# The chunked two-way scan of a recurrent mixer moved to four quadrants of the array, with its five operand products on GpSimd

## Chip, cores, metric

One core of a Trainium2 chip runs the whole network in one launch. The metric is the device time of that launch in microseconds (us). PE is TensorE (PEld its weight loads), DVE is VectorE, ACT is ScalarE, POOL is GpSimd, SP issues the DMAs.

## The reference, cut to what matters

The program is a network of several blocks. The edit lies in one mixer of the second part, an RWKV-7 style recurrence over 256 context and then 512 latent tokens, 8 heads of 64, once forward and once backward:

```
def _rwkv7_scan(S0, r, w, k, v, kk, a):
    def step(S, inp):
        r_t, w_t, k_t, v_t, kk_t, a_t = inp
        sa = jnp.einsum('bhvk,bhk->bhv', S, kk_t)
        S = (S * w_t[:, :, None, :] - sa[..., None] * (kk_t * a_t)[:, :, None, :]
             + v_t[..., None] * k_t[:, :, None, :])
        return S, jnp.einsum('bhvk,bhk->bhv', S, r_t)
```

`yf_l` and `yb_l` of the two directions are added, normalised per head, and gated. Everything is fp32.

## The kernel before, in words

`rwkv_prepare` computes the decays' running sums (`cum`), the normalised keys (`kk`) and their negative product with `a` (`b_neg`) for all 769 columns (256, a gap, 512). `rwkv_scan` then goes over 12 chunks of 64 tokens in each direction, and `rwkv_finish` adds, normalises and gates. Each is a phase of its own, with a barrier at its ends.

In the scan the 8 heads lie as 4 column groups (`q`) by two halves of 64 partitions. A matmul of one head has 64 rows, 64 columns and 64 moving columns, and in fp32 it is two instructions in the trace. `heads` puts the two halves' heads on the two diagonal quadrants of the array: rows 0 to 63 write to partitions 0 to 63, rows 64 to 127 to partitions 64 to 127.

A chunk of one direction is a chain of steps, in the list `order`:

- ScalarE `grown`: the exponentials of the running sum and of its negative (`own`, `grow`, L2697, L2698); `identity` refills the 512-column start of the doubling (L2700)
- VectorE `bent`: four products of 256 columns that bend kk, k, b and r by them (L2734 to L2737)
- TensorE `scores`: five score products a head; VectorE masks them (L2741, L2746) and starts the solve (L2743)
- TensorE `turned` and ScalarE `tm`: k, b and v token-major (L2705, L2706)
- five doubling levels of a triangular inverse: TensorE `y`, ScalarE copy `yl` (L2709), TensorE `p`, VectorE `x`, a one-column copy to `bearer` (L2751) and a predicated copy of 512 columns (256 in the last) under the level's mask (L2754)
- `g`, `u`, `out` and the state `s`: the chunk's right side, the solved vectors, outputs and the new state (L2758, L2712, L2715, L2763, L2765).

All steps but the masks of the scores wait for one another. The two directions are independent; each engine's queue is written out by `run`: steps of direction 0, and of direction 1 with a lag of 16 entries, one after the other. An engine takes its queue in order, so a step of one direction that waits holds back the other's step behind it. The scan's buffers (chunk operands, `zx`, `yl`, token-major copies, state) lie in the weight ring; direction d owns four PSUM banks.

Of the kernel before, what the change touches and what calls it, by code (L numbers as in the profile page):

```python
# [25 lines left out]
def _const_table():  # L26
# [47 lines left out]
    put("before", row < to)  # L74
    put("after", row > to)
    put("until", row <= to)
    put("since", row >= to)
# [2328 lines left out]
def rwkv_prepare(kit, f, w_dram, pick_dram, pack2, cum, kk, b_neg, small_cols, squares):  # L2406
# [14 lines left out]
    def col(name, c):  # L2421
# [3 lines left out]
    loaded, bent, summed, taken, squared, ksummed, stepped, rooted, ones_less, inverted, spread, decayed = (  # L2425
        ph.sem(f"rw_{s}") for s in
        ("loaded", "bent", "summed", "taken", "squared", "ksummed", "stepped", "rooted", "ones_less", "inverted",
         "spread", "decayed"))
# [106 lines left out]
def rwkv_scan(kit, f, cum, kk, b_neg, y_out, decays, bearer):  # L2535
# [3 lines left out]
    one = 256  # L2539
# [4 lines left out]
    used = 0  # L2544

    def take(n):
        nonlocal used
        used += n * one
        return kit.ring[:, used - n * one:used].rearrange("p (q n) -> p q n", n=64)

    dirs = []
    for d in range(2):
        t = Dir()
        t.fwd = d == 0
        t.kk, t.k, t.b, t.r = (take(1) for _ in range(4))
        t.grow, t.v_chunk, t.v_tok, t.state, t.u = (take(1) for _ in range(5))
        t.auk_n, t.zx, t.k_b_tok, t.rk_rb = (take(2) for _ in range(4))
        t.z, t.x, t.auk, t.n_t = t.zx[:, 0:4], t.zx[:, 4:8], t.auk_n[:, 0:4], t.auk_n[:, 4:8]
        t.k_tok, t.b_tok, t.rk, t.rb = t.k_b_tok[:, 0:4], t.k_b_tok[:, 4:8], t.rk_rb[:, 0:4], t.rk_rb[:, 4:8]

        t.yl, t.g0 = t.b, t.u
# [3 lines left out]
        t.end = 64 if t.fwd else 0  # L2565
        t.strict = kit.const("before" if t.fwd else "after")
        t.inclusive = kit.const("until" if t.fwd else "since")
        t.bearer = bearer[:, d:d + 1]
        t.bank = 4 * d
        t.cum, t.y = cum[d], y_out[d]  # L2570
        t.merge = [kit.const(f"merge{l}")[:, 64 * d:64 * d + P] for l in range(6)]
        dirs.append(t)

    order = [("act", "grown"), ("act", "identity"), ("dve", "bent"), ("pe", "scores"), ("act", "v_copied"),
             ("dve", "masked"), ("dve", "aux"), ("pe", "turned"), ("act", "tm"),
             ("pe", "y1"), ("pe", "g"), ("act", "yl1"), ("pe", "p1"), ("dve", "g0"), ("dve", "x1")]
    for l in range(2, 6):
        order += [("pe", f"y{l}"), ("act", f"yl{l}"), ("pe", f"p{l}"), ("dve", f"x{l}")]
    order += [("pe", "u"), ("act", "u"), ("pe", "out"), ("act", "y"), ("dve", "s")]
    pe_names, act_names, dve_names = ([n for e, n in order if e == engine] for engine in ("pe", "act", "dve"))  # L2580

    for t in dirs:
        t.pe = Steps(ph.sem("scan_pe"), *pe_names)
        t.act = Steps(ph.sem("scan_act"), *act_names)
        t.dve = Steps(ph.sem("scan_dve"), *dve_names)
    lag = 4 * 4
    chunks = (CTX // 64, SEQ // 64)

    def run(engine, step):


        def turn(i, part, leading=True, trailing=True, before=None):

            started = part * chunks[0]
            for k in range(len(order)):
                if leading and order[k][0] == engine:
                    step(dirs[0], i, part, i + started, order[k][1])
                at = k - lag
                if at < 0 and before is not False and order[at][0] == engine:
                    j, p = before or (i - 1, part)  # L2600
                    step(dirs[1], j, p, j + p * chunks[0], order[at][1])
                if at >= 0 and trailing and order[at][0] == engine:
                    step(dirs[1], i, part, i + started, order[at][1])

        turn(0, 0, before=False)
        for i in range(1, chunks[0]):
            turn(i, 0)
        turn(0, 1, before=(chunks[0] - 1, 0))
        for i in range(1, chunks[1]):
            turn(i, 1)  # L2610
        turn(0, 1, leading=False, trailing=False, before=(chunks[1] - 1, 1))

    zeroed = [ph.sem("scan_zeroed") for _ in dirs]

    for t in dirs:
        t.mid = ph.sem("scan_mid")

    def banks(t, k, n=4, at=0):

        flat = ps[:, t.bank + k:t.bank + k + 2, :].rearrange("p b n -> p (b n)") if at + n > 8 else ps[:, t.bank + k, :]  # L2620
        return flat[:, at * 64:(at + n) * 64].rearrange("p (q n) -> p q n", n=64)

    def offset(t, part, i):

        n, at = (CTX // 64, 0) if part == 0 else (SEQ // 64, CTX + 1)
        return i * 64 + at if t.fwd else i * -64 + (at + 64 * (n - 1))

    with ph as block:
        @block.tensor
        def _(pe):  # L2630
            def heads(out, terms):

                for q in range(4):
                    for n, (lhs, rhs) in enumerate(terms):
                        for half in HALVES:
                            mm = pe.matmul(out[half, q, :], lhs[half, q, :], rhs[half, q, :],  # L2636
                                           start=(n == 0), stop=(n == len(terms) - 1))
                return mm

            def turned(out, x):  # L2640
                same = kit.const("stack")
                for q in range(4):
                    for half in HALVES:
                        mm = pe.matmul(out[half, q, :], x[half, q, :], same[half, :], start=True, stop=True)
                return mm

            def step(t, turn, name):
                wait = lambda s, n: pe.wait_ge(s.done, s.value(turn, n))
                if name == "scores":
                    wait(t.dve, "bent")  # L2650
                    wait(t.act, "grown")
                    heads(banks(t, 0, at=0), [(t.k, t.kk)])
                    heads(banks(t, 0, at=4), [(t.b, t.kk)])
                    heads(banks(t, 1), [(t.kk, t.b)])
                    heads(banks(t, 3, at=0), [(t.k, t.r)])
                    mm = heads(banks(t, 3, at=4), [(t.b, t.r)])
                elif name == "turned":
                    wait(t.dve, "aux")
                    wait(t.act, "v_copied")
                    turned(banks(t, 1, at=0), t.k)  # L2660
                    turned(banks(t, 1, at=4), t.b)
                    mm = turned(banks(t, 2), t.v_chunk)
                elif name == "g":
                    wait(t.act, "tm")
                    mm = heads(banks(t, 3), [(t.auk, t.v_tok), (t.kk, t.state)])
                elif name[0] == "y":
                    l = int(name[1:])
                    if l > 1:
                        wait(t.dve, f"x{l - 1}")
                    mm = heads(banks(t, 0), [(t.n_t, t.x)])  # L2670
                elif name[0] == "p":
                    wait(t.act, f"yl{name[1:]}")
                    mm = heads(banks(t, 1, at=0), [(t.yl, t.z)])
                    if name != "p5":
                        mm = heads(banks(t, 1, at=4), [(t.z, t.yl)])
                elif name == "u":
                    wait(t.dve, "x5")
                    mm = heads(banks(t, 2), [(t.z, t.g0)])
                elif name == "out":
                    wait(t.act, "u")  # L2680
                    heads(banks(t, 3), [(t.k_tok, t.v_tok), (t.b_tok, t.u)])
                    mm = heads(banks(t, 0), [(t.state, t.r), (t.v_tok, t.rk), (t.u, t.rb)])
                mm.then_inc(t.pe.done, 1)

            for t in dirs:
                pe.wait_ge(zeroed[dirs.index(t)], 1)
                pe.transpose(ps[:, t.bank, 0:P], kit.const("ident"), kit.const("ident")).then_inc(t.pe.done, 1)
# [1184 lines left out]
```

## Time and profile before

| | us |
|---|---|
| median of 3 runs | 4436.44 (4434.1 to 4438.89) |
| profiled execution, first to last instruction | 4435.9 |
| preparation of the mixer, 2337.1 to 2398.5 | 61.4 |
| scan, 2398.5 to 2864.5 | 466.0 |
| finish, 2864.5 to 2906.5 | 42.0 |
| TensorE busy in the scan | 375.9 |
| VectorE, ScalarE, GpSimd busy in the scan | 193.8, 120.6, 0 |

Times of the trace are microseconds from the start of the span. Busy time of TensorE counts a matmul from its start to its modelled end, and matmuls overlap. The granted clock is a share of 2.4 GHz.

### The profile page before, as it was taken

The page shows a single profiled execution, that of the slowest core. Times are in us where ns is not written, and L with a number is a line of the kernel's source. Part 1 is how long each engine was busy: PE and PEld are TensorE (multiplying, and loading weights), DVE is VectorE, ACT ScalarE, POOL GpSimd, SP SyncE. Part 2 cuts the span into 40 slices and gives each one's busy share as a digit, 9 for nine tenths or more (in the row PEclk, how much of TensorE's full clock was granted, in tenths as well). Part 3 has the DMA queues.
Part 4 walks back from the last instruction along what each step waited for, and adds up shares of the span by engine and source line. Part 5 has one row for each costly group of instructions (what it writes and reads, how often), then busy time and mean ns, then how long its engine had stood idle before and what let it go on. Part 6 is the DMA issues. An engine that isn't in the chain of part 4 may idle for free. (4 is left out here: it accounts for less than half of the span.)

```text
span 4435.9 us, 69845 instructions
## 1 busy us (share of the span) xinstructions
PE 3930.5 (89%) x29200; PEld 3231.3 (73%) x29200; DVE 2140.0 (48%) x3431; ACT 1412.1 (32%) x2577; POOL 32.2 (1%) x52
## 2 busy tenths in 40 slices
PE   7989999989899999968794888889999989768998
PEld 5767777767667777756683777777888877656887
DVE  5575644444766544343545444444333336575334
ACT  3234432222335322233523222223211233363222
POOL 0000000000000000000000000000000000000000
PEclk8999999999899999979997999989999999889999
DMA  5332444423424444310010000011212121002222
GB/s 151 98 95 62 136 156 158 162 97 92 107 60 140 140 145 143 123 57 6 20 48 5 3 3 3 24 38 57 62 62 66 38 72 52 1 20 74 91 92 85
DMA packets 311231, 337.87 MB, mean 76 GB/s; under 512 B 23552, under 2 KB 289568, under 8 KB 304416
## 3 DMA queue, kind: packets, MB, share of 16 engines
q1 hardware_dynamic: 310272, 329.45, 23.5%
q10 hardware_dynamic: 672, 4.36, 0.4%
q8 instruction: 209, 3.42, 0.3%
q14 instruction: 78, 0.64, 0.0%
HBM read 314.91 MB, written 18.87 MB: 75 GB/s over the span
## 5 line engine op out<-in xcount | busy, mean ns | idle before, releaser
L276 DVE TENSOR_TENSOR weights_lo<-weight_ring,weights_hi 128x1024 fp32r<-128x1024 f32 x371 | 454.5, 1225 | 1375.8 <-ACT weights_hi L272 1375.8
L272 ACT ACTIVATE weights_hi<-weight_ring 128x1024 fp32r<-128x1024 f32 x371 | 392.8, 1059 | 1605.9 <-PE banks L323 1534.5
L323 PE MATMUL banks<-mlp_x_lo,weights_hi 128*128 128x512 f32 (+1 forms) x1280 | 479.8, 375 | 0.0
L323 PE MATMUL banks<-mlp_hidden_hi,weights_hi 128*128 128x512 f32 (+1 forms) x1280 | 477.1, 373 | 0.0
L323 PE MATMUL banks<-mlp_hidden_lo,weights_hi 128*128 128x512 f32 (+1 forms) x1280 | 476.4, 372 | 0.0
L323 PE MATMUL banks<-mlp_hidden_hi,weights_lo 128*128 128x512 f32 (+1 forms) x1280 | 475.9, 372 | 0.0
L2636 PE MATMUL banks<-weight_ring 64*64 64x64 f32 x10368 | 341.9, 221 | 86.3 <-DVE weight_ring L2754 45.7
L2636 PEld LDWEIGHTS banks<-weight_ring 64*64 64x64 f32 x10368 | 321.0, 137 | 105.4 <-DVE weight_ring L2754 52.8
L323 PE MATMUL banks<-normed_hi,weights_hi 128*128 128x512 f32 (+1 forms) x1040 | 360.8, 347 | 21.8 <-ACT normed_hi L290 19.7
L323 PE MATMUL banks<-mlp_x_hi,weights_hi 128*128 128x512 f32 x768 | 307.2, 400 | 21.5 <-DVE mlp_x_lo L307 9.5
L323 PE MATMUL banks<-mlp_x_hi,weights_lo 128*128 128x512 f32 x768 | 304.9, 397 | 0.0
L323 PEld LDWEIGHTS banks<-mlp_hidden_hi,weights_hi 128*128 128x128 f32 x1280 | 240.9, 188 | 52.1 <-issue 6.7
L323 PEld LDWEIGHTS banks<-mlp_x_lo,weights_hi 128*128 128x128 f32 x1280 | 242.4, 189 | 45.0
L323 PEld LDWEIGHTS banks<-mlp_hidden_hi,weights_lo 128*128 128x128 f32 x1280 | 240.7, 188 | 45.7
L323 PEld LDWEIGHTS banks<-mlp_hidden_lo,weights_hi 128*128 128x128 f32 x1280 | 240.8, 188 | 45.2
L323 PE MATMUL banks<-normed_hi,weights_lo 128*128 128x256 f32 x736 | 250.0, 340 | 0.0
L323 PEld LDWEIGHTS banks<-normed_hi,weights_hi 128*128 128x128 f32 x1040 | 197.4, 190 | 52.1 <-issue 20.1
L1069 PE MATMUL banks<-scaled_hi,weights_hi 128*128 128x512 f32 x416 | 181.2, 436 | 32.8 <-PEq L147 15.5
L323 PEld LDWEIGHTS banks<-mlp_x_hi,weights_hi 128*128 128x128 f32 x768 | 145.7, 190 | 69.0 <-DVE weights_lo L276 20.5
L323 PEld LDWEIGHTS banks<-mlp_x_hi,weights_lo 128*128 128x128 f32 x768 | 145.7, 190 | 34.7
L1069 PE MATMUL banks<-scaled_lo,weights_hi 128*128 128x512 f32 x416 | 170.4, 410 | 0.0
L1069 PE MATMUL banks<-scaled_hi,weights_lo 128*128 128x512 f32 x416 | 169.9, 408 | 0.0
(531 smaller groups left out, 6823.8 us busy)
## 6 DMA issues: line engine op xcount, KB each, us to landing
weight_ring<-in_w SPq DMA_DIRECT2D x64, 1024.0 KB, 5.6
mod_chunks<-in_mod_w SPq DMA_DIRECT2D x24, 2048.0 KB, 10.6
weight_ring<-in_w_in SPq DMA_DIRECT2D x42, 1024.0 KB, 5.3
weight_ring<-in_w_up SPq DMA_DIRECT2D x32, 1024.0 KB, 6.0
weight_ring<-in_w_down SPq DMA_DIRECT2D x32, 1024.0 KB, 5.2
weight_ring<-in_w_in SPq DMA_DIRECT2D x52, 512.0 KB, 4.2
weight_ring<-in_w_out SPq DMA_DIRECT2D x16, 1024.0 KB, 5.7
gate_logits_dram<-gates_staged SPq DMA_DIRECT2D x48, 256.0 KB, 4.4
```

The lines of the kernel that those rows point to most:

```text
L272: act.activation(self.w_hi[:, t % 2], self._raw(t), ACT.Copy).then_inc(self.w_rounded, 1)
L276: dve.tensor_tensor(self.w_lo[:, t % 2], self._raw(t), self.w_hi[:, t % 2].bitcast(F32), ALU.subtract)\
L323: mm = pe.matmul(bank, a[:, k, :], b[:, k, t0:t0 + w], start=(k == 0 and n == 0), stop=(k == KD - 1 and n == 2))
L1069: mm = pe.matmul(self.banks[n % 2], w[:, k, :], x[:, k, :], start=(k == 0 and m == 0), stop=(k == KD - 1 and m == 2))
L2636: mm = pe.matmul(out[half, q, :], lhs[half, q, :], rhs[half, q, :], start=(n == 0), stop=(n == len(terms) - 1))
```

## The change

The scan is written anew; preparation and finish gain four DMAs each.

- The matmuls are written so that a step uses all four 64x64 quadrants where it can: a head's data crosses from one half of the partitions to the other and back (`other`). Work that had been a step by itself is laid into the doubling levels as a second product (`a`, `b` banks in `apply`). The k and b of a chunk sit side by side (`kb`: k, b, k), so one product with 128 columns and 128 moving columns (`join`) gives all scores that need masks, and 8 transposes of 64x128 turn k and b.
- The identity start and the five `yl` are filled once, and later chunks rewrite only the masked places.
- In a doubling level VectorE makes the narrow predicated copy (`keep`, 256 columns) and ScalarE the wide plain one (`merge`, 512 columns); before it was the other way round.
- The products that bend the operands are five (k twice) and stand on GpSimd, in `bend` (kk and b, which `cross` reads) and `bend_rest` (k, k, r, which `join` reads). They are in the order list between the last level of a chunk and the next chunk's start.
- `grow`, `bend`, `cross`, `start`, `join` and `mask` of the next chunk stand ahead of the end of the list, so they are issued with the current chunk's last steps. ScalarE also takes the chunk's end decay.
- The new buffers need more room than the ring, so the first half of `mixed` (128 x 4 x 768 fp32, 1.57 MB) is used too: its contents are stored to DRAM in four DMAs of the preparation and loaded back in four of the finish.
- The steps are ordered by `order`, 36 entries, and direction 1 lags by 18.

```
 rwkv_prepare, on SP, behind the four loads:
+            for c in range(4):
+                sp.dma_start(kept[c], aside[:, c, :]).then_inc(set_aside, 16)
             sp.wait_ge(loaded, 64)
+            sp.wait_ge(set_aside, 64)
 rwkv_finish, on SP:
             sp.dma_start(g2, g2_dram).then_inc(loaded, 16)
+            for c in range(4):
+                sp.dma_start(aside[:, c, :], kept[c]).then_inc(restored, 16)
             following(sp)
             sp.wait_ge(loaded, 16)
+            sp.wait_ge(restored, 64)
 rwkv_scan:
+    order = [("pe", "apply", 1, 0), ("dve", "keep", 1, 0), ("pe", "turn", 0, 0), ("pe", "grow_by", 1, 0),
+             ("act", "token_major", 0, 0), ("act", "merge", 1, 0)]
+    for l in range(2, 5):
+        order += [("pe", "apply", l, 0), ("dve", "keep", l, 0), ("pe", "grow_by", l, 0), ("act", "merge", l, 0)]
+    order += [("pe", "apply", 5, 0), ("act", "grow", 0, 1), ("dve", "keep", 5, 0), ("pe", "grow_by", 5, 0),
+              ("dve", "g", 0, 0), ("act", "merge", 5, 0), ("pool", "bend", 0, 1), ("pe", "solve", 0, 0),
+              ("act", "u", 0, 0), ("pool", "bend_rest", 0, 1), ("pe", "state", 0, 0), ("pe", "out", 0, 0),
+              ("dve", "state", 0, 0), ("pe", "cross", 0, 1), ("act", "y", 0, 0), ("dve", "start", 0, 1),
+              ("pe", "join", 0, 1), ("dve", "mask", 0, 1)]
+    lag = len(order) // 2
...
 TensorE (one() is a matmul; heads() yields q, h, half, other):
+            def apply(t, l, turn):
...
+                for q, h, half, other in heads():
+                    mm = one(out[half, q, :], t.scored[other, h, q, 0:64], x[other, q, :])
+                    if l == 2:
+                        mm = one(t.a[half, 1, q, :], t.scored[half, h, q, 0:64], t.v_tok[half, q, :], start=q == 0)
+                    if l == 3:
+                        mm = one(t.a[half, 0, q, :], t.kb_tok[half, h, q, :], t.v_tok[half, q, :], start=False)
+                    if l == 4:
+                        mm = one(t.b[half, 1, q, :], t.v_tok[half, q, :], t.scored[half, h, q, 64:P], start=q == 0)
+                    if l == 5:
+                        mm = one(t.a[half, 1, q, :], t.kr[half, q, 0:64], t.state[half, q, :], start=False)
+                mm.then_inc(t.applied[l], 1)
+            def grow_by(t, l, turn):
+                z = t.first[:, 0] if l == 1 else t.zx[:, 0]
+                pe.wait_ge(t.kept[l], turn + 1)
+                for q, h, half, other in heads():
+                    mm = one(t.c[half, 0, q, :], t.yl[l][half, q, :], z[half, q, :])
+                    if l < 5:
+                        mm = one(t.d[other, 0, q, :], z[half, q, :], t.yl[l][half, q, :])
+                mm.then_inc(t.grown_by[l], 1)
+                if l == 5:
+                    for q, h, half, other in heads():
+                        mm = one(t.b[half, 1, q, :], t.state[half, q, :], t.kr[half, q, 64:P], start=False)
+                    mm.then_inc(t.read, 1)
...
 cross:
+                    for q, h, half, other in heads():
+                        one(t.c[half, 0, q, :], t.kb[half, q, 64:P], t.kr[half, q, 0:64])
+                        mm = one(t.d[other, 0, q, :], t.kr[half, q, 0:64], t.kb[half, q, 64:P])
 join:
+                    for q, h, half, _ in heads():
+                        mm = one(t.ab[:, h, q * P:(q + 1) * P], t.kb[half, q, 64 * h:64 * h + P], t.kr[half, q, :])
 turn:
+                    for q, h, half, _ in heads():
+                        pe.transpose(t.ab[:, h, q * 64:(q + 1) * 64], t.kb[half, q, 64 * h:64 * h + P], same[half, :])
+                    for q, h, half, _ in heads():
+                        mm = one(t.a[half, 1, q, :], f[half, RW_V + q, at:at + 64], same[half, :])
 solve, state, out: 8 matmuls each, into c, a and b
...
 GpSimd:
+                if name == "bend":
+                    pool.wait_ge(t.grown, turn + 1)
+                    if turn:
+                        pool.wait_ge(t.turned, turn)
+                        pool.wait_ge(t.applied[5], turn)
+                    pool.tensor_tensor(t.kr[:, :, 0:64], kk[:, :, at:at + 64], t.before, ALU.mult)
+                    pool.tensor_tensor(t.kb[:, :, 64:P], b_neg[:, :, at:at + 64], t.grow, ALU.mult).then_inc(t.bent, 1)
+                elif name == "bend_rest":
+                    if turn:
+                        pool.wait_ge(t.read, turn)
+                    pool.tensor_tensor(t.kb[:, :, 0:64], f[:, RW_K:RW_K + 4, at + 1:at + 65], t.grow, ALU.mult)
+                    pool.tensor_tensor(t.kb[:, :, P:192], f[:, RW_K:RW_K + 4, at + 1:at + 65], t.grow, ALU.mult)
+                    pool.tensor_tensor(t.kr[:, :, 64:P], f[:, RW_R:RW_R + 4, at + 1:at + 65], t.own,
+                                      ALU.mult).then_inc(t.rest_bent, 1)
 VectorE:
+                if name == "start":
...
+                    dve.tensor_copy(t.bearer, kit.const("ones")[:, 0:1])
+                    dve.copy_predicated(t.first, t.merge[0].unsqueeze(2).broadcast_to([P, 2, 4, 64]),
+                                        t.cd[:, :, 0:256].rearrange("p m (q n) -> p m q n", q=4)).then_inc(t.started, 1)
+                elif name == "mask":
+                    dve.wait_ge(t.joined, turn + 1)
+                    dve.tensor_tensor(t.scored.rearrange("p h q n -> p (h q) n"),
+                                      t.ab.rearrange("p h (q n) -> p (h q) n", q=4), over(t.seen, 8),
+                                      ALU.mult).then_inc(t.masked, 1)
+                elif name == "keep":
+                    dve.wait_ge(t.applied[l], turn + 1)
+                    dve.tensor_copy(t.bearer, kit.const("ones")[:, 0:1])
+                    dve.copy_predicated(t.yl[l], t.merge[l][:, 1:2].broadcast_to([P, 4, 64]),
+                                        t.d[:, 1]).then_inc(t.kept[l], 1)
...
 ScalarE:
+                elif name == "merge":
+                    act.wait_ge(t.grown_by[l], turn + 1)
+                    n = 1 if l == 5 else 2
+                    act.activation(t.zx[:, 0:n].rearrange("p m q n -> p m (q n)"), t.cd[:, 0:n, 0:256],
+                                   ACT.Copy).then_inc(t.merged[l], 1)
```

## Rows read from the trace of the kernel before

**Rows 1.** The page: span, and each engine's busy time with its share and instructions.
```profile
span 4435.9 us, 69845 instructions
...
PE 3930.5 (89%) x29200; PEld 3231.3 (73%) x29200; DVE 2140.0 (48%) x3431; ACT 1412.1 (32%) x2577; POOL 32.2 (1%) x52
```

**Rows 2.** Windows: preparation, scan, finish, the other scan; last columns granted clock, DMA share, GB/s.
```profile
2337.10:2398.50 61.40, 19.99 (x80) 10.75 (x80) 45.21 (x50) 27.12 (x43) 0.00 (x0) 0.62 0.03 8
2398.50:2864.50 466.00, 375.86 (x11522) 355.49 (x11522) 193.84 (x484) 120.56 (x315) 0.00 (x0) 0.98 0.01 3
2864.50:2906.50 42.00, 34.32 (x144) 25.88 (x144) 28.44 (x50) 8.14 (x11) 0.00 (x0) 0.80 0.18 57
3890.00:4100.00 210.00, 155.21 (x853) 133.17 (x854) 130.84 (x311) 107.56 (x270) 3.29 (x6) 0.87 0.15 46
```

**Rows 3.** Waits of the scan: who for whom, total us, times, longest.
```profile
DVE rw_small L2751 <- PE banks L2636: 163.0, 86, 4.1
...
PE banks L2636 <- DVE weight_ring L2754: 45.7, 52, 1.2
```

**Rows 4.** Groups of the scan: count, then busy us, mean ns, idle before.
```profile
L2636 PE MATMUL banks<-weight_ring 64*64 64x64 f32 x10368 | 341.9, 221 | 86.3 <-DVE weight_ring L2754 45.7 <-ACT weight_ring L2709 28.2 <-DVE weight_ring L2737 10.6
...
L2741 DVE TENSOR_TENSOR weight_ring<-banks,consts 128x512 f32<-128x512 f32 x24 | 16.6, 691 | 56.6 <-PE banks L2636 56.6
...
L2705 ACT ACTIVATE weight_ring<-banks 128x512 f32<-128x512 f32 x24 | 14.3, 597 | 52.9 <-PE banks L2644 52.9
L2754 DVE COPY_PREDICATED weight_ring<-consts,banks 128x256 f32<-128x256 uint32 x24 | 10.4, 432 | 0.0
...
L2734 DVE TENSOR_TENSOR weight_ring<-rw_kk,rw_decays 128x256 f32<-128x256 f32 x24 | 10.0, 418 | 11.2 <-ACT weight_ring L2698 11.2
```

**Rows 5.** Timeline of one turn of the scan: start us, duration us.
```profile
2592.68 0.72 DVE L2743 COPY_PREDICATED weight_ring<-consts,banks 128x512 f32<-128x512 uint32 x1
...
2596.89 5.81 PE L2636 MATMUL banks<-weight_ring 64*64 64x64 f32 x192 [0.32 <-ACT weight_ring L2709]
...
2599.95 0.15 DVE L2751 COPY rw_small<-consts 128x1 f32<-128x1 f32 x1 [0.97 <-PE banks L2636]
2600.02 0.73 DVE L2754 COPY_PREDICATED weight_ring<-consts,banks 128x512 f32<-128x512 uint32 x1
...
2605.22 0.68 PE L2636 MATMUL banks<-weight_ring 64*64 64x64 f32 x16 [0.89 <-DVE weight_ring L2754]
...
2605.95 0.38 ACT L2709 ACTIVATE weight_ring<-banks 128x256 f32<-128x256 f32 x1 [1.50 <-PE banks L2636]
...
2629.95 0.72 DVE L2743 COPY_PREDICATED weight_ring<-consts,banks 128x512 f32<-128x512 uint32 x1
```

**Rows 6.** TensorE's groups of the whole span: a product on four column strips.
```profile
L2520 PE MATMUL banks<-rw_y_back,consts 128*32 128x512 f32 x8 | 1.1, 592 | 0.0
```

**Rows 7.** Timeline, three places: a change of array form, a GpSimd product's neighbour, 128-column products.
```profile
242.64 1.13 PE L1179 MATMUL banks<-window_side,projected 64*128 64x256 f32 x8
243.71 0.66 PE L1189 MATMUL banks<-window_side,weight_ring 128*128 128x64 f32 x4
...
2048.22 0.69 DVE L2322 TENSOR_TENSOR weight_ring<-banks,axial 128x512 f32<-128x512 f32 x1 [0.17 <-PE banks L2296]
...
3905.12 0.60 PE L3445 MATMUL banks<-consts,weight_ring 128*64 128x128 f32 x4
```

**Rows 8.** Lines of two products: minimum/median/maximum ns, first and last start us.
```profile
L2312 POOL TENSOR_TENSOR diff_proj<-diff_proj,axial x8: 1269/1274/1754, 2041.7 to 2051.5; 128x512 f32<-128x512 f32 x8
...
L2326 DVE TENSOR_TENSOR diff_proj<-diff_proj,weight_ring x8: 678/680/1771, 2049.7 to 2056.1; 128x512 f32<-128x512 f32 x8
```

**Rows 9.** DMA of the finish (2864.5 to 2907 in 40 slices), and its queue.
```profile
GB/s 2 200 348 379 370 352 352 210 9 0 0 0 0 0 0 0 0 15 0 0 0 0 0 0 0 0 0 0 0 0 0 0 0 0 0 0 0 0 0 0
...
q1 hardware_dynamic: 2224, 2.36, 17.5%
```

More of the change, by code:

```diff
@@ L73, in _const_table @@
     row, to = i[:, None] % 64, np.arange(64)[None, :]
[L74 to L77, printed above, removed]
+    put("seen_fwd", np.concatenate([row < to, row <= to], 1))
+    put("seen_back", np.concatenate([row > to, row >= to], 1))
     for l in range(6):
@@ L2532, with rwkv_scan, take @@
 HALVES = (slice(0, 64), slice(64, 128))
-def rwkv_scan(kit, f, cum, kk, b_neg, y_out, decays, bearer):
+def rwkv_scan(kit, f, cum, kk, b_neg, y_out, decays, small, spare):
     nc, ph, ps = kit.nc, kit.ph, kit.ps
-    one = 256
+    turns, first = T2 // 64, CTX // 64
     class Dir:
         pass
[L2544 to L2549, printed above, removed]
+    rooms, used = (kit.ring, spare), [0, 0]
+    def take(*dims):
+        n = 64 * math.prod(dims)
+        r = 0 if used[0] + n <= RING_FLOATS else 1
+        used[r] += n
+        flat = rooms[r][:, used[r] - n:used[r]]
+        if len(dims) == 1:
+            return flat.rearrange("p (q n) -> p q n", q=dims[0])
+        return flat.rearrange("p (h q n) -> p h q n", h=dims[0], q=dims[1])
     dirs = []
@@ L2554, in rwkv_scan @@
         t.fwd = d == 0
[L2555 to L2561, printed above, removed]
+        t.kb, t.kr = take(12).rearrange("p (q m) n -> p q (m n)", m=3), take(8).rearrange("p (q m) n -> p q (m n)", m=2)
+        t.scored = take(2, 8).rearrange("p h (q m) n -> p h q (m n)", m=2)
+        t.first = take(2, 4)
+        t.zx = take(2, 4)
+        t.yl = [None] + [take(4) for _ in range(5)]
+        t.kb_tok = take(2, 4)
+        t.v_tok, t.state, t.g0, t.u = (take(4) for _ in range(4))
+        t.grow = t.zx[:, 1]
         t.decay = decays[:, d]
@@ L2577, in rwkv_scan @@
[L2577 to L2586, printed above, removed]
@@ L2587, in rwkv_scan @@
-    chunks = (CTX // 64, SEQ // 64)
-    def run(engine, step):
[L2592 to L2625, printed above, removed]
+        t.last = 63 if t.fwd else 0
+        t.bearer = small[:, d:d + 1]
@@ new lines, in rwkv_scan @@
+        t.ends = [small[:, 4 + 8 * d + 4 * e:8 + 8 * d + 4 * e] for e in range(2)]
+        t.seen = kit.const("seen_fwd" if t.fwd else "seen_back")
+        t.merge = [kit.const(f"merge{l}")[:, 64 * d:64 * d + P].rearrange("p (m n) -> p m n", m=2).bitcast(mybir.dt.uint32)
+                   for l in range(6)]
+        t.cum, t.y = cum[d], y_out[d]
+        t.a, t.b, t.c, t.d = (ps[:, 4 * d + n, :].rearrange("p (m q n) -> p m q n", m=2, q=4) for n in range(4))
+        t.ab, t.cd = ps[:, 4 * d:4 * d + 2, :], ps[:, 4 * d + 2:4 * d + 4, :]
@@ new lines, in rwkv_scan, with offset @@
+    lag = len(order) // 2
+    def run(engine, step):
+        own = [(on, name, l, turn + ahead) for turn in range(-1, turns) for on, name, l, ahead in order]
+        for k in range(len(own) + lag):
+            for t, at in zip(dirs, (k, k - lag)):
+                if 0 <= at < len(own) and own[at][0] == engine and 0 <= own[at][3] < turns:
+                    step(t, *own[at][1:])
+    def offset(t, turn):
+        n, at, i = (first, 0, turn) if turn < first else (turns - first, CTX + 1, turn - first)
@@ L2630, in _, with one, heads @@
         def _(pe):
-            def heads(out, terms):
+            same = kit.const("stack")
+            def one(out, lhs, rhs, start=True):
+                return pe.matmul(out, lhs, rhs, start=start, stop=True, skip_group_check=True)
+            def heads():
                 for q in range(4):
[L2634 to L2678, printed above, removed]
-                elif name == "out":
[L2680 to L2683, printed above, removed]
@@ L2685, in _ @@
[L2685 to L2688 removed]
+                    for h in range(2):
+                        yield q, h, HALVES[h], HALVES[1 - h]
+            def apply(t, l, turn):
+                x = t.first[:, 1] if l == 1 else t.zx[:, 1]
+                out = t.d[:, 1]
+                if l == 1:
+                    pe.wait_ge(t.started, turn + 1)
+                    pe.wait_ge(t.masked, turn + 1)
+                else:
+                    pe.wait_ge(t.merged[l - 1], turn + 1)
+                if l == 2:
+                    pe.wait_ge(t.token_major, turn + 1)
+                if l == 5 and turn:
+                    pe.wait_ge(t.decayed, turn)
+                if l == 5 and not turn:
+                    pe.wait_ge(t.emptied, 1)
+                for q, h, half, other in heads():
+                    mm = one(out[half, q, :], t.scored[other, h, q, 0:64], x[other, q, :])
+                    if l == 2:
+                        mm = one(t.a[half, 1, q, :], t.scored[half, h, q, 0:64], t.v_tok[half, q, :], start=q == 0)
[6 more added lines that the diff above has]
+                mm.then_inc(t.applied[l], 1)
@@ L2718, in _ @@
+                    act.activation(t.y(at, 0 if turn < first else 1), t.b[:, 1], ACT.Copy).then_inc(t.y_copied, 1)
             for t in dirs:
-                one = t.decay[:, :, 0:1] if t.fwd else t.decay[:, :, 64:65]
-                act.activation(one, kit.const("ones")[:, 0:4].unsqueeze(2), ACT.Copy).then_inc(t.act.done, 1)
-            run("act", lambda t, i, part, turn, name: step(t, turn, offset(t, part, i), part, name))
+                outer = t.decay[:, :, 0:1] if t.fwd else t.decay[:, :, 64:65]
@@ L2777, in rwkv_finish @@
+            for t in dirs:
+                dve.memset(t.state, 0.0).then_inc(t.emptied, 1)
+            for t in dirs:
+                dve.wait_ge(t.emptied, 1)
+            run("dve", step)
+def rwkv_finish(kit, f, g2_dram, pack2, y_f, y_b, scratch, following, aside, kept):
     nc, ph, ps = kit.nc, kit.ph, kit.ps
```

183 lines of the change are left out of this document (98 added, 85 removed).

## The prediction

> **What bounds the kernel now.** I read the page first [rows 1]: one core, 4435.9 us of span, and TensorE carries the kernel. That is an average over stages, so I cut the trace at the phase borders [rows 2]. Only three phases are edited. The preparation takes 61.4 us, the scan 466.0 us, the finish 42.0 us. In the scan TensorE has a record open for 375.9 of 466.0 us, VectorE for 193.8, ScalarE for 120.6, GpSimd for nothing; the granted clock is 0.98, the 2.4 GHz level.
>
> The waits of the scan [rows 3] tell a chain: VectorE waits for TensorE (VectorE's wide merge alone 163.0 us), TensorE waits far less (45.7 us for that merge). TensorE's rate comes first, the handovers second. The rate is in the timeline [rows 5]: 192 instructions took 5.81 us, less the 0.22 us that one of them lasts [rows 4], so 29.1 ns each. They go two at a time, one on each diagonal quadrant of the array, so a quadrant takes a new instruction every 58 ns. A chunk has 240 matmuls of two instructions, 480; 24 chunks make 11,520 of the 11,522 in [rows 2]. A turn (a chunk in each direction) thus costs TensorE 960 x 29.1 ns = 27.9 us. The turn itself is 2629.95 - 2592.68 = 37.3 us [rows 5]: 28 us of array and 9 us of handovers that the other direction doesn't cover.
>
> **Units of the handovers** [rows 4, 5]. A burst of 16 instructions that waited lasts 0.68 us from start to last result; the next engine starts 0.05 us later. Two instructions that follow each other without a wait overlap, by 0.08 to 0.1 us. A predicated copy starts 0.07 us behind its bearer copy and lasts 0.43 us for 256 columns and 0.73 for 512, a ScalarE copy 0.38 us for 256 columns and 0.60 for 512, the masking product 0.69 us for 512.
>
> With these I laid the four queues of a program side by side in their written order, each instruction starting when its queue and what it waits for allow. For the kernel before this gives 37.2 us a turn (measured 37.3) and 457 us for the scan; the trace has 466. The 9 us between are the phase's opening, its 1.3 us table load and its close. I add them to every walk below.
>
> **The change, part by part.**
>
> *TensorE.* A chunk now has 208 matmuls of two instructions and 8 transposes of one. Nine steps (levels 2 to 5 of apply, 1 to 4 of grow_by, cross) hold 16 matmuls that go over all four quadrants, 8 instructions in each: 8 x 58 ns = 0.46 us for 32 instructions. Six steps (apply 1, grow_by 5, the read behind it, solve, state, out) use two quadrants: 16 instructions, 0.46 us as well. The join has 128-column weights and 128 moving columns; four such in a row last 0.60 us, so an instruction takes 0.11 us beyond the first one's 0.27 [rows 7], two row halves side by side, 8 each: 0.87 us. The turn is 4 transposes per row half, 0.44 us, and 0.46 us for the values. Sum 15 x 0.46 + 0.87 + 0.90 = 8.7 us a chunk, 17.5 a turn.
>
> Whether all four quadrants run at once no row shows. Near it: four column strips of a 512-column product ran together, 8 instructions of 592 ns in 1.1 us [rows 6], and the two diagonal quadrants do already. Lower bound 58/4 = 14.5 ns an instruction, upper bound 29 ns (no gain from the second pair). I take 14.5: each axis overlaps by itself, and a burst is short.
>
> *Shape changes of the array.* Turn and join leave the 64x64 form and come back. Going from 128x128 to 64x128 and back [rows 7], 8 instructions in four rounds of 0.21 us should need 0.85 us; from first start to the next form's start it was 1.07. I take 0.15 us a change, four a chunk (bounds 0 and 0.2).
>
> *VectorE.* It loses four products of 0.42 us a chunk [rows 4] and three masking and identity steps of 0.68 to 0.72, and gains one mask of 1,024 columns (1.25 us by the same slope) and a 512-column start copy; the four wide merges shrink from 512 to 256 columns. About 5 us a chunk against 8, never the bound.
>
> *ScalarE* trades four 256-column copies for 512-column merges: 4.7 us a chunk, covered.
>
> *GpSimd.* Five products of 256 columns. The nearest row is 1.27 us for 512 [rows 8], so 0.64 to 1.27; I take 0.8, or 4.0 us a chunk. The growth is ready just after apply 5, bend's two products have until cross, some 6 us on, bend_rest until join, 9 us on. In the walk nothing changes up to 1.4 us a product; at 2.0 a turn gains 1.6 us. So the move itself costs nothing but contention: the VectorE product with both inputs in SBUF took 0.68 us alone and 1.77 beside GpSimd's, which went from 1.27 to 1.75 [rows 8]; a product with one input in PSUM stayed at 0.69 beside them [rows 7]. In the new scan the second state product has both inputs in SBUF, and the bearer copy reads and writes SBUF. In the walk two or three copies a turn fall on a GpSimd product: 0 to 1 us a turn. I take 0.5.
>
> This agrees with the Trainium skill (GPSIMD Engine Reference, Key points), which says that GpSimd shares its SBUF interfaces with VectorE, so that an instruction with two SBUF inputs or in a two-port mode contends. By the page's other rule (section 4.1, elementwise work belongs on VectorE, GpSimd being about twice as slow) the move would be a loss; the rows have 1.27 against 0.69, and with every product uncovered it would be worth 24 x 5 x 0.4 = 48 us.
>
> *The DMAs.* Four stores of 0.4 MB in the preparation and four loads in the finish, on SP's queue. The preparation moves 8 GB/s in the mean of its 61 us [rows 2]; the finish moved 2.36 MB at up to 379 GB/s within 10 us of its 42 [rows 9]. 1.57 MB more is 5 us, over long before the finish ends. The four issues delay the first weights by 2 us and those 5, again under cover. Cost nothing; uncovered, 5 to 7 us. GpSimd's clearing of some 80 semaphores lies in the finish too.
>
> **The walk of a turn.** The directions run half a turn apart. A half turn in which direction 0 goes through levels 1 to 4:
> - apply 1, the other's apply 5, turn with two shape changes, token-major copies, merge 1: 0.51 + 0.46 + 1.20 + 0.21 + 0.80 + 0.52 + 0.13 = 3.83
> - levels 2 and 3: (0.67 + 0.05 + 0.50 + 0.05 + 0.67 + 0.05 + 0.60 + 0.05) = 2.64 each, 5.28, and 0.11 behind the other direction's cross
> - apply 4, keep 4, grow_by 4: 0.72 + 0.55 + 0.51 = 1.78
> - the other's join, queued behind it, its mask, and its apply 1 can start: 1.17 + 0.26 + 1.17 + 0.13 = 2.73
>
> That is 13.7 us. In the other half the join stands ahead of grow_by 4, which saves 1.27: 12.5 us. A turn is 26.3 us, of which TensorE issues for 18.7. The first apply 1 starts at 13.0; 11 turns, the half-turn lag and 16.6 us of last chunk make 13.0 + 289.0 + 13.8 + 16.6 = 332 us. With 9 us of edges and 12 x 0.5 of contention: 347. The scan shrinks by 466 - 347 = 119 us. Against the profiled span of 4435.9 that is 4317; the runs' median of 4436.4 differs by 0.5 us, so **4317 us**.
>
> **The rivals.**
> - *Four quadrants are no faster than two* (issue or the array at 29 ns an instruction): the same walk gives 32.5 us a turn, 407 us, so 422 with edges and contention, 4392. Half of it, at 22 ns, gives 370, so 385, 4355. For it: no matmul of this size comes faster than every 29.1 ns in any row, and a turn has 848 of them now, 960 before. Against: the strips of [rows 6]. Chance 0.27, for both together. The Trainium skill (TensorE: Matmul & The Clock Gate, Part 1) puts the start-to-start time of matmuls at no less than about 25 ns, however small they are. By that rule the walk gives 385 us, and an estimated 4370. The 29.1 ns agrees with it as a mean; the strips, eight of 592 ns in 1.1 us, do not tell, since they are long.
> - *GpSimd's port lock bites on every keep.* At worst VectorE stands for all 8 us of GpSimd's work in a turn: 12 x 7.5 more, 4407. For it the 1.77 us; against it, the copies' main input lies in PSUM. Chance 0.06.
> - *The clock falls.* In the other scan, of 128-row products, TensorE was busy for 74% by its records and the granted clock was 0.87 [rows 2]. Should the new bursts leave the clock at 1.2 GHz, instructions cost double: 37.8 us a turn, 471 us in the walk, 4456, slower than before. It decides from about 37 us a turn, so only if nearly the whole scan runs at that level. Against it: issue fills 71% of a turn, it was 75%, and no gap is over 1.1 us. Chance 0.04.
> - *The likeliest*, all as walked: 0.63. Its own range is 4290 (no cost for shape changes or contention, two-quadrant steps overlapping the next) to 4345.
>
> **Numbers.** The range 4288 to 4394 takes in the first rival whole and leaves out the other two, 0.1, and a gain beyond the lower bounds, 0.08. Anything under 0.2% (9 us) is no change that this kernel's measurement can tell. Faster 0.94: the likeliest, the first rival, and 0.04 of the second. Same 0.02: the rest of the second, should it come on top of the first. Slower 0.04: the clock.
>
> **What would show it.** The scan phase at some 345 us; start to start of one direction's apply 1 near 26 us; a burst of 32 instructions on four quadrants no longer than one of 16 had been, 0.68 us; granted clock over 0.95; GpSimd products near 0.8 us, ended before TensorE's cross and join wait for them; bearer copies well over 0.15 us where they meet a GpSimd product; preparation and finish at 61 and 42 us. The prediction is wrong if a burst of 32 takes 1.15 us, or if TensorE's waits name GpSimd.

## The result, and the profile after

The changed kernel takes 4318.14 us (median of 4 runs, 4313.11 to 4323.36) against 4435.27 beside it: ratio 0.9735, 95% interval 0.9721 to 0.9749. Predicted were 4317. Its profiled span is 4318.7 us.

The windows, as [rows 2]: preparation, scan, finish; the columns end with granted clock, DMA share, GB/s.

```profile
2336.00:2398.00 62.00, 19.98 (x80) 10.73 (x80) 45.38 (x51) 27.15 (x43) 0.00 (x0) 0.62 0.09 33
2398.00:2745.00 347.00, 271.00 (x10176) 239.84 (x10176) 132.23 (x386) 125.29 (x303) 79.76 (x120) 0.94 0.02 4
2745.00:2787.00 42.00, 32.73 (x144) 23.76 (x144) 28.51 (x50) 9.22 (x13) 0.00 (x0) 0.81 0.29 94
```

The whole gain is the scan's, 466 to 347 us; all the rest of the span is longer by 1.8 us. Preparation and finish keep their length (61.4 and 62.0 us, 42 and 42) while they move more bytes (8 to 33 GB/s, 57 to 94).

The groups of the scan, by shape (count, then busy us, mean ns, idle before), against [rows 4]. The narrow predicated copy is still 0.43 us, the one mask of 1,024 columns 1.22 (1.25 forecast), the wide plain copy on ScalarE 0.60, a GpSimd product 0.69 (0.8 forecast).

```profile
L2794 DVE COPY_PREDICATED weight_ring<-consts,banks 128x256 f32<-128x256 uint32 x72 | 30.6, 432 | 0.0
L2788 DVE TENSOR_TENSOR weight_ring<-banks,consts 128x1024 f32<-128x1024 f32 x24 | 29.4, 1224 | 25.7 <-PE banks L2624 25.7
L2737 ACT ACTIVATE weight_ring<-banks 128x512 f32<-128x512 f32 x48 | 28.7, 599 | 62.3 <-PE banks L2624 62.2
...
L2771 POOL TENSOR_TENSOR weight_ring<-rw_features,rw_decays 128x256 f32<-128x256 f32 x24 | 16.5, 686 | 0.0
```

The timeline, as [rows 5], at a mask (L2788): 32 instructions over four quadrants last 0.69 us, as long as 16 over two did (0.68). Their starts come four at a time, 7 ns apart, and a new four every 58 ns: each quadrant keeps its pace, and all four run. Then the same step of the next turn, 26.35 us later.

```profile
2520.50 0.69 PE L2624 MATMUL banks<-mixed 64*64 64x64 f32 x32
2520.61 1.22 DVE L2788 TENSOR_TENSOR weight_ring<-banks,consts 128x1024 f32<-128x1024 f32 x1 [0.72 <-PE banks L2624]
...
2546.85 0.68 PE L2624 MATMUL banks<-mixed 64*64 64x64 f32 x27
2546.97 1.23 DVE L2788 TENSOR_TENSOR weight_ring<-banks,consts 128x1024 f32<-128x1024 f32 x1 [0.57 <-PE banks L2624]
2547.81 0.34 PE L2624 MATMUL banks<-mixed 64*64 64x64 f32 x5 [0.29 <-issue]
```

The second burst breaks after 27 of 32 instructions and goes on 0.5 us later. No engine is named behind it ("issue"): TensorE waited for nothing that the profile shows. In the scan of the kernel before TensorE has no such wait; here it has ten, of 0.2 to 0.7 us.

Windows of whole turns, from one mask of direction 0 to its next: the first, the second, and the one after that break.

```profile
2410.10:2440.80 30.70, 24.06 (x711) 21.23 (x715) 9.40 (x28) 7.68 (x17) 4.36 (x7) 0.68 0.01 3
2440.80:2467.20 26.40, 21.43 (x856) 19.07 (x860) 11.01 (x33) 9.94 (x24) 6.59 (x10) 1.00 0.02 4
...
2547.00:2574.40 27.40, 22.40 (x856) 19.66 (x856) 10.92 (x33) 9.94 (x24) 6.67 (x10) 1.00 0.02 4
```

The undisturbed turn is 26.4 us, half turns 13.7 and 12.7. The first has the granted clock at 0.68 in the mean (1.2 GHz until 2429.6 us, 2.4 from there), and some later ones are up to 1.2 us longer at full clock with the same work in them.

Instructions themselves come by DMA. The scan's queues, first before, then after:

```profile
q8 instruction: 90, 1.47, 1.3%
```

```profile
q8 instruction: 80, 1.31, 1.5%
```

1.31 MB in 80 packets are 16,384 bytes each. TensorE has 2 x 10,176 instructions in the scan (a weight load and a product each), so a packet is about 254 of them (256 before, by 90 packets and 2 x 11,522). That is one packet every 5.2 us before (466/90) and every 4.3 us now. Where bursts break, they break some 127 products apart or a multiple of that (the 3,763rd, 3,890th and 4,017th from 2430 us on), which is 254 instructions. A burst broken there goes on 1.2 to 1.6 us after a packet has landed. The break at 2547.3, in the DMA view of 2544 to 2550 (40 slices of 0.15 us; a packet shows in the slice in which it starts): a packet starts at 2544.9 and lands at 2546.3, TensorE goes on at 2547.8, the next packet starts at 2549.4.

```profile
GB/s 0 0 0 0 0 109 0 0 0 0 0 0 0 0 0 0 0 0 0 0 0 0 0 0 0 0 0 0 0 0 0 0 0 0 0 0 109 0 0 0
...
q8 instruction: 2, 0.03, 2.5%
```

So I formed a second theory (B) beside the walk (A, the order of the queues sets the turn): the array now empties blocks of instructions nearly as fast as they come.

### The profile page after: what moved, and what is told of

The parts are those of the page before. It is cut to its first block and busy times, and to the rows that moved or that the text cites. A ratio compares the mean times of both kernels' runs of the same rounds, so it can differ in the third digit from the quotient of the medians.

```text
span 4318.7 us, 67312 instructions
## 1 busy us (share of the span) xinstructions
PE 3826.1 (89%) x27854; PEld 3116.1 (72%) x27854; DVE 2077.7 (48%) x3333; ACT 1416.6 (33%) x2565; POOL 111.9 (3%) x172
## 5 line engine op out<-in xcount | busy, mean ns | idle before, releaser
L2624 PE MATMUL banks<-weight_ring 64*64 64x64 f32 (+1 forms) x5952 | 177.8, 233 | 79.6 <-POOL weight_ring L2765 35.9
L2624 PEld LDWEIGHTS banks<-weight_ring 64*64 64x64 f32 (+1 forms) x5952 | 151.7, 144 | 98.0 <-POOL weight_ring L2765 37.5
L321 PEld LDWEIGHTS banks<-mlp_x_hi,weights_hi 128*128 128x128 f32 x768 | 145.7, 190 | 69.1 <-DVE weights_lo L274 20.5
```

The lines of the kernel that those rows point to most:

```text
L321: mm = pe.matmul(bank, a[:, k, :], b[:, k, t0:t0 + w], start=(k == 0 and n == 0), stop=(k == KD - 1 and n == 2))
L2624: return pe.matmul(out, lhs, rhs, start=start, stop=True, skip_group_check=True)
```

## Experiments

All start from the changed kernel; its 4318.14 us is the number to compare with. Ratios are to the kernel before.

**1. Two quadrants instead of four** (two_quadrants)

```
-  mm = one(out[half, q, :], t.scored[other, h, q, 0:64], x[other, q, :])      # apply, l > 1
+  mm = one(out[half, q, :], same[half, :], x[half, q, :])
-  mm = one(t.d[other, 0, q, :], z[half, q, :], t.yl[l][half, q, :])           # grow_by
+  mm = one(t.d[half, 0, q, :], same[half, :], t.yl[l][half, q, :])
```
(and the same in `cross`)

> The products that had their weights in the off-diagonal quadrants in apply 2 to 5, grow_by 1 to 4 and cross are put on the two diagonal ones, as many instructions as before; what is computed there is no longer the scan, and the output is scaled down to stay finite. Theory (the gain comes from four quadrants running at once): a burst of 32 instructions takes about 1.15 us instead of 0.69, the walk with 29 ns an instruction gives 32.3 us a turn instead of 26.1 and a scan of 347 + 75 = 422 us, so 4385 to 4395 us. Rival (the gain comes from fewer instructions and another order, the quadrants don't matter): within 5 us of 4318.

4384.71 us, ratio 0.9889 [0.9874, 0.9904]. Its scan, and the first and last of the eight groups in which one burst of 32 shows:

```profile
2398.00:2810.00 412.00, 351.46 (x10176) 326.72 (x10176) 132.12 (x386) 126.41 (x303) 79.86 (x120) 0.98 0.01 3
```

```profile
2541.58 0.34 PE L2624 MATMUL banks<-mixed 64*64 64x64 f32 x4
...
2542.45 0.33 PE L2624 MATMUL banks<-mixed,consts 64*64 64x64 f32 x4
```

From 2541.58 to 2542.78 are 1.20 us for the burst, and every middle turn is 32.65 us (walk 32.3). The four quadrants are worth 412 - 347 = 65 us of the 119. The walk said 75; 8 of the missing 10 are what the faster kernel has more of: 4.7 us by which its later turns are over the undisturbed one, and 4.3 us of slow clock in the first turn against 0.9 (33.56 less 32.65). The other 54 us of the 119 no run takes apart. By the walk, not by a run, they come from fewer instructions (848 a turn for 960) and fewer handovers, and it fits both ends: 37.2 us a turn against 37.3 in the kernel before, 32.3 against 32.65 here.

**2. What GpSimd's part is worth** (bend_vector, pool_twice, pool_three)

```
-  ("pool", "bend", 0, 1) ... ("pool", "bend_rest", 0, 1)        # bend_vector
+  ("dve", "bend", 0, 1) ... ("dve", "bend_rest", 0, 1)
```
```
+  for _ in range(n - 1):                                         # pool_twice, pool_three
+      made[0] += 1
+      pool.tensor_tensor(out, a, b, ALU.mult).then_inc(again, 1)
+      pool.wait_ge(again, made[0])
   return pool.tensor_tensor(out, a, b, ALU.mult)
```

> The five bending products of a chunk go back to VectorE, at the same place of the order; all else as changed. Theory (VectorE has slack, the handovers between TensorE, VectorE and ScalarE set the turn): the walk gives 328 us against 330, turn 26.1 as before, so 4312 to 4322 us, with VectorE busier by 120 x 0.42 = 50 us. Rival (VectorE is what the move relieved): those 50 us come back, 4350 to 4368 us.

> Each GpSimd product is made twice, one after the other, the second behind a wait for the first. Theory (GpSimd is hidden up to 1.4 us a product): about 1.45 us a product, the walk gives 4 us more at the scan's opening and the same turn, so 4318 to 4326 us, bearer copies still 0.15 us. Rival (GpSimd is near its limit, or takes VectorE's port): 5 x 0.7 x 24 = 84 us of products more, at least a third of it shown, 4345 us or more, and bearer copies or state products longer.

> Each GpSimd product is made three times, each behind a wait for the last. Theory: about 2.2 us a product is beyond the slack, TensorE's cross and join wait for GpSimd, the walk gives 29.7 us a turn and 47 us more, so 4350 to 4380 us. Rival (GpSimd has no part in the turn at any length tried): 4318 to 4330 us.

| | us | ratio | scan |
|---|---|---|---|
| bend_vector | 4316.90 | 0.9733 [0.9719, 0.9746] | 343.6 |
| pool_twice | 4323.06 | 0.9749 [0.9734, 0.9764] | 347.9 |
| pool_three | 4371.69 | 0.9857 [0.9842, 0.9872] | 398.0 |

With the products on VectorE that engine is busy for 173.2 us instead of 132.2, and the time is the same: the move to GpSimd is worth nothing here. Twice the products hide too, but for 4.9 us in all (4 were expected, at the scan's opening). Three times don't, and then the waits of TensorE (2450 to 2800) begin with GpSimd:

```profile
PE banks L2624 <- POOL weight_ring L2764: 27.7, 17, 2.2
PE banks L2624 <- ACT mixed L2737: 14.5, 33, 0.7
```

TensorE idles more there, the scan's granted clock is 0.88 for 0.94, and part of the 51 us may be that; how much isn't shown.

**3. The lag** (lag_28, lag_11)

```
-    lag = len(order) // 2        # 18
+    lag = 28                     # or 11
```

> One number of the changed kernel is different: the second direction follows the first by 28 steps of the written order instead of 18. Nothing else, the same instructions. Theory A (each engine's written queue sets the turn: who stands behind whom): the walk gives 24.2 us a turn instead of 26.1 and 17 us less for the scan, 330 us, so 4301 us. Theory B, which comes on top (TensorE's instructions arrive in blocks of 16,384 bytes, 80 of them in the scan, never less than 3.4 us apart; a turn uses 6.7): at 24.2 us a block would be wanted every 3.6 us, so more pauses inside a burst at the ends of blocks, up to 10 us given back, 4301 to 4311 us. Rival (work of the array sets the turn, the order doesn't matter): 4318 us.

> The same with 11 steps instead of 18. Theory A: the walk gives 25.4 us a turn and 13 us less for the scan, 4305 us. Rival (the order doesn't matter): 4318 us.

4318.75 us, 0.9733 [0.9720, 0.9746], and 4315.30, 0.9726 [0.9711, 0.9741]. Theory A alone falls; B with at most 10 us given back was too small, since with lag 28 all 17 are gone. The waits of TensorE that name no engine in the scan, changed kernel, then lag 28:

```profile
PE banks L2624 <- issue: 4.3, 10, 0.7
```

```profile
PE banks L2624 <- issue: 17.4, 33, 1.2
```

Behind the first turn, lag 28 has turns from 25.05 to 27.93 us and lag 11 from 26.68 to 28.28; the walk had 24.2 and 25.4. For lag 28 all eleven are 28 us over the walk (294.1 against 266), 18 more than in the changed kernel; 13 of these 18 are such waits, the rest isn't traced to one.

The place of the breaks is the same everywhere: in the eight kernels with all their instructions that have such waits, 124 in all, they fall within 8 products of the same place in a count by 127, and TensorE goes on 1.2 to 1.6 us after a packet has landed.

**4. DMA traffic beside the scan** (spill)

```
+  for turn in range(turns):
+      for n, t in enumerate(dirs):
+          sp.wait_ge(t.masked, turn + 1)
+          for c in range(4):
+              sp.dma_start(spill[8 * turn + 4 * n + c], kk[:, c, 0:T2]).then_inc(spilled, 16)
```

> In the scan of the changed kernel SyncE stores 96 x 0.39 MB to DRAM, four stores behind each mask, which nothing waits for but the phase's end; no engine gets an instruction more. Theory B (TensorE's instructions come by DMA and late ones stop it inside a burst): the 16 KB blocks land later beside the stores, more than 1.0 us each, more pauses of 0.3 to 1 us at block ends, so 5 to 40 us more, 4323 to 4358 us, and the turns of the slowed chunks get longer without any engine waiting for another. Rival (the pauses have another cause, DMA traffic is free here as the prediction took the four stores of the preparation to be): within 4 us of 4318.

4337.79 us, 0.9782 [0.9767, 0.9797]: 20 us more, with no other engine's work changed, and TensorE stopped in bursts like this one:

```profile
2446.39 0.34 PE L2634 MATMUL banks<-weight_ring 64*64 64x64 f32 x7 [0.94 <-issue]
```

One point of the expectation was wrong: an instruction packet itself still took 1.05 us in the mean (1.05 without the stores). Since TensorE goes on 1.2 to 1.6 us after a landing here too, the delay lies before the packet starts. The granted clock also falls to 1.2 GHz four times for 3.4 us between 2440 and 2625, where the changed kernel has no fall.

**5. Half the instructions, the same columns** (pairs, pairs_28, pairs_11, pairs_spill)

```
-  for q, h, half, other in heads():
-      mm = one(t.c[half, 0, q, :], t.yl[l][half, q, :], z[half, q, :])
+  for q, w, h, half, other in pairs():        # w = slice(q, q + 2), q = 0, 2
+      mm = one(t.c[half, 0, w, :], t.yl[l][half, q, :], z[half, w, :])
```
(and the same in every 64x64 step but the values' turn)

> In the changed kernel's 64x64 steps one matmul of 128 moving columns takes the place of two of 64: as many columns on each quadrant, half the instructions. The weights of every second head are left out, so what is computed is no longer the scan; the output is scaled down to stay finite. 18 steps of lag, as changed. Theory B (TensorE's instruction blocks come too late now and then): some 45 blocks of 16,384 bytes in the scan instead of 80, no pause inside a burst, all middle turns alike, 26.1 us by the walk, up to 1.5 us more if the last instruction of a burst, twice as long, delays each handover; no turn longer than the others. Rival (the pauses have another cause): turns still scatter by 1 us as in the changed kernel.

> The same with 28 steps of lag. With half the instruction blocks the walk's order effect should come out whole if it is true: theory A and B together: 1.9 us a turn less than in the run with 18 steps, 17 us less for the kernel. Rival (the order doesn't matter, the walk is wrong about 28 steps, as its run with all instructions could also mean): the same time as with 18 steps.

> The same with 11 steps of lag. Theories A and B together: 0.75 us a turn less than with 18 steps, 13 us less for the kernel. Rival: the same time as with 18 steps, or more, as its undisturbed turns of 26.7 us with all instructions suggest.

> The run with matmuls of 128 moving columns (half the instructions, 18 steps of lag) with the 96 stores of 0.39 MB in the scan as well. Theory B: the stores cost turns only by way of late instruction blocks, and with 45 blocks instead of 80, some 7 us apart, there is time to spare: turns of 25.8 us as without the stores, within 4 us of that run's 4309. Rival (the stores slow SBUF reads, the clock or something else): turns 2 us longer, as they were with all instructions, 4325 us or more.

| | us | ratio | scan | middle turns |
|---|---|---|---|---|
| pairs | 4308.83 | 0.9713 [0.9697, 0.9729] | 334.4 | 25.82 to 25.83 |
| pairs_28 | 4286.80 | 0.9666 [0.9650, 0.9682] | 312.6 | 23.37 to 23.38 |
| pairs_11 | 4287.64 | 0.9669 [0.9653, 0.9686] | 315.4 | 24.97 to 24.99 |
| pairs_spill | 4306.14 | 0.9706 [0.9690, 0.9722] | 334.3 | 25.82 to 25.83 |

The scan of pairs, its packets, and the scan of pairs_spill with its stores at 115 GB/s:

```profile
2404.00:2738.40 334.40, 257.24 (x5568) 205.40 (x5568) 131.71 (x386) 125.17 (x303) 79.81 (x120) 0.94 0.01 2
```

```profile
q8 instruction: 44, 0.72, 0.9%
```

```profile
2398.40:2732.70 334.30, 257.22 (x5568) 205.43 (x5568) 131.65 (x386) 125.19 (x303) 79.80 (x120) 0.94 0.30 115
```

The array does the same columns (burst of 16 instructions of 128 columns: 0.67 us), and no wait without an engine is left from 2440 to 2700 in any of the four. The scatter is gone, and the stores cost nothing. The lags now give more than the walk said: 2.5 and 0.85 us a turn (expected 1.9 and 0.75), 22 and 21 us in all (expected 17 and 13). With lag 11 some 4 us of that are the clock's and not the order's: it is at 2.4 GHz from 2418.9 us instead of 2435.6, which takes 2.6 us off the first turn beyond the 0.85, and it doesn't fall in the last chunk, which is 1.7 us shorter. Theories A and B hold together: the order sets the turn, and the supply of instructions hides it in the kernel with all of them. Halving the instructions would also relieve TensorE if it were slow in taking them by itself; against that stand the place of the breaks and the stores, which cost 20 us with all instructions and nothing with half.

These four kernels don't compute the scan, since every second head's weights are left out. Their times show a cause, not a gain that this scan could have.

**6. A warm start** (warm)

```
+  if name == "cross" and not turn and t is dirs[0]:
+      for n in range(80):
+          one(t.a[HALVES[n % 2], 0, n // 2 % 4, :], kit.const("stack")[HALVES[n % 2], :], same[HALVES[n % 2], :])
```

> 80 small matmuls with constants are put ahead of the first direction's first cross, where TensorE of the changed kernel stands idle for 8 us; nothing reads their result. Theory C (the opening's turn is slow since the granted clock is at 1.2 GHz until 2429.6, 24 us later than in the kernel before): the clock rises at or before the first apply 1, the first turn is 26.4 us instead of 30.7, the scan 343 instead of 347, 4314 us. Rival (the first turn is long for another reason): scan 347 us, 4318 us. The ends of the 16 KB blocks also shift by 320 instructions: by theory B the pauses inside bursts then fall on other steps than in the changed kernel, still some 254 instructions apart.

4318.74 us, 0.9735 [0.9722, 0.9748]: nothing. Four windows of its opening and the rest:

```profile
2396.00:2400.30 4.30, 4.14 (x78) 4.17 (x80) 0.54 (x2) 4.16 (x14) 0.00 (x0) 0.50 0.01 2
2400.30:2407.10 6.80, 4.27 (x136) 3.98 (x132) 0.79 (x2) 3.07 (x8) 4.34 (x7) 1.00 0.01 2
2407.10:2427.60 20.50, 15.42 (x364) 13.45 (x360) 5.15 (x12) 4.09 (x9) 2.43 (x5) 0.50 0.01 2
2427.60:2737.60 310.00, 250.18 (x9771) 221.76 (x9768) 126.16 (x370) 113.90 (x273) 73.09 (x110) 1.00 0.02 4
```

The clock rose at 2400.3, before cross, and fell again at 2407.1, after the extra matmuls had ended (2402.9) and TensorE had stood idle for 1.3 and 1.2 us in the first chunk's handovers; the first turn was 31.0 us. The first turn is the long one wherever the clock is low in it (1.2 GHz over most of it and 30.7 us in the changed kernel; up at 2415.9 and 33.56 for 32.65 in experiment 1), so theory C holds in that. It was wrong that one push keeps the clock up. The profiled scan was 5 us shorter for other reasons (no fall of the clock at its end, fewer late blocks), and the runs' median doesn't show it.

Its other expectation came true. The five breaks left between 2440 and 2700 (1.0 us of waits; 3.2 in the changed kernel) come with the 2,774th, 5,316th, 7,223rd, 7,858th and 7,985th product, the 160 extra ones counted: multiples of 127 apart as before, and at the same place in the count, so at other steps of the scan.

## Why the prediction was right, by its steps

- **Four quadrants at once:** shown, 14.5 ns an instruction in a burst, and 65 us by experiment 1. The rivals of 22 to 29 ns fall. The Trainium skill (TensorE: Matmul & The Clock Gate, Part 1) has some 25 ns as the least start-to-start time; over four quadrants the trace has a mean of 14.5 ns, and the measurement decides.
- **The walk:** half turns 13.7 and 12.5 forecast, 13.7 and 12.7 measured. The join with its two changes of form, forecast at 1.17 us, takes 1.24: 0.15 us into it, 0.89 from its first to its last start (2533.08 to 2533.97), 0.20 out of it. The changes at the turn take 0.15 us each. Opening 13.0 against 13.5.
- **Contention:** the term of 0.5 us a turn is the step that was wrong: 0. The bearer copy takes 132 to 155 ns at all 120 places, the 44 beside a GpSimd product too, and the state product never meets a GpSimd product in this order. The mechanism is real all the same. The second state product's duration (minimum/median/maximum ns), changed kernel, then lag 28, where it falls beside GpSimd in one direction:

```profile
L2803 DVE TENSOR_TENSOR mixed<-mixed,rw_small x12: 424/425/427, 2450.2 to 2744.5; 128x256 f32<-128x256 f32 x12
```

```profile
L2803 DVE TENSOR_TENSOR mixed<-mixed,rw_small x12: 424/797/806, 2456.8 to 2745.8; 128x256 f32<-128x256 f32 x12
```

  By the Trainium skill (GPSIMD Engine Reference, Key points) such a two-input product contends with GpSimd; the trace agrees, 0.43 against 0.80 us.
- **The sum:** 332 of walk + 9 of edges + 6 of contention gave 347, and 347 was measured, but with other contents. Of the 6 us of contention nothing is there, and of the 9 of edges, taken over from the kernel before, 2.4 at the opening and in the last chunk. The opening is 0.5 longer than walked, the eleven turns 9.9 (298.9 against 289.0), the half-turn lag 2.1, the last chunk 1.9: 14.4 us. In the turns it is 4.3 us of the first one, most of it at 1.2 GHz, 4.7 us in which late instruction blocks show (the other ten are 26.83 in the mean, 26.36 undisturbed), and 0.1 us a turn of the walk. Lag and last chunk include two short falls of the clock:

```profile
2723.20:2726.60 3.40, 3.05 (x52) 2.67 (x52) 1.22 (x1) 0.54 (x1) 0.00 (x0) 0.50 0.00 0
2740.20:2743.60 3.40, 2.92 (x60) 2.73 (x58) 0.04 (x1) 0.77 (x2) 0.00 (x0) 0.50 0.02 5
```

  That the two sums agree to the microsecond is luck; the walk alone, without edges and contention, would have said 4302.
- **GpSimd:** 0.69 us a product instead of 0.8, hidden. TensorE's waits name it twice, both times at the opening (2406.1 and 2408.0 us), where nothing can cover it. It hides at twice the length and shows at three times, as walked (limit between 1.4 and 2.0).
- **The clock:** 0.94, just under the 0.95 asked for, all of it at the ends of the scan. The rival of a whole scan at 1.2 GHz did not come.
- **DMAs:** free as forecast, since they lie outside the scan. Inside it stores cost 20 us (experiment 4), which the prediction's reasoning on hidden transfers would have missed.

Open stays how far ahead instruction blocks are asked for, what each part of the rewrite other than the quadrants and GpSimd is worth, and how the 20 us of experiment 4 divide between late blocks and the short falls of the clock that come with the pauses.

## What to carry to other kernels

Lay an in-order kernel's queues side by side before editing: here the walk gave each half turn to 0.2 us, and it showed that relieving VectorE is worth nothing while it has slack. Small matmuls gain from all four quadrants even in short bursts, but count instructions as well: once TensorE wants a 16 KB block every 4 us or so, a better order gains nothing until the same columns are done with fewer instructions. Where a longer moving side can replace two short ones under the same weights, do that first, and keep bulk DMAs out of such a stretch.

## What was not expected of the hardware

- TensorE's instructions arrive in packets of 16,384 bytes; two of them never started less than 3.2 us apart in the scan of any run. At one per 4.3 us in the mean TensorE already idles for 0.2 to 0.7 us inside bursts, by no engine's doing; at one per 5.2 (the kernel before) it doesn't.
- 38 MB of stores beside the scan made those breaks longer (13.4 us of waits without an engine between 2440 and 2700, 3.2 without the stores) and did nothing to a kernel with half the instructions.
- In experiment 6 the granted clock fell back to 1.2 GHz after 6.8 us in which TensorE had a record open for 4.3 and no gap was over 1.3 us, and it stayed there for 20.5 us in which TensorE had one open for 15.4.
